# Moving the sample states' part of the delta rule beside the last prompt tile's gathers, and the cache pages to GpSimd's queue

## The reference

```python
q, k, v, qkv_b, z, b_raw, a_raw = project(rmsnorm(h), w_in)   # 1024 -> 3592 columns
oa = diff_attention(q, k, v)            # samples also read 8 pages x 128 keys and values of a paged cache each
q, k, v, g, beta = conv4_silu(qkv_b)    # four-tap causal convolution, then the decays
ob, S_new = gdn_chunk(S, q, k, v, g, beta)   # chunked delta rule; a sample sequence is one chunk of 8 tokens
#   rhs   = beta (v - e^G k S);  delta = solve(I + A, rhs)
#   ob    = e^G q S + (decay qk) delta
#   S_new = e^Gl S + delta^T (e^(Gl-G) k)
h = h + merge(oa, ob * silu(z)) @ w_out
# PEER: 8 heads choose 16 of 16384 experts each; one row of u and one of v per choice
h = h + sum_k gate_k gelu(xn . u[e_k]) v[e_k]
```

## Time and profile before

| | |
|---|---|
| runs, us | 2124.64, 2133.01, 2137.26 (median 2133.01) |
| profiled execution, us | 2127.18, of which the span is 2125.5 |
| busy | TensorE 81%, VectorE 63%, ScalarE 38%, GpSimd 37% |
| bytes | HBM read 762.27 MB, written 16.26 MB |
| first slot's dot product starts | 531.4 us into the span |

### The profile page before, as it was taken

The page is one execution under the profiler, slowest core; times in us unless marked ns, Lnnn a source line. Parts: engine busy times, 40 slices in busy tenths (PEclk is TensorE's granted clock), DMA queues, the critical chain, the costliest instruction groups (busy, mean ns, idle before and its releaser), DMA issues.

```text
span 2125.5 us, 20551 instructions
## 1 busy us (share of the span) xinstructions
PE 1728.4 (81%) x6211; PEld 864.8 (41%) x6211; DVE 1335.3 (63%) x3023; ACT 799.8 (38%) x2370; POOL 783.6 (37%) x704
## 2 busy tenths in 40 slices
PE   6886999998898887989788889978796667776877
PEld 1332454546453444445344435533452223443111
DVE  2333534334797656887665788865687876669654
ACT  1332321222544523563443345463243333323433
POOL 2132100012344443435334343634443554444442
PEclk8898999999998989999899999999897888888999
DMA  9797843226999999999999999999999999999997
GB/s 347 269 348 256 263 139 114 74 104 232 405 424 401 426 428 428 426 423 408 427 408 429 425 426 399 416 414 415 427 426 411 427 427 429 427 426 426 426 427 316
DMA packets 137479, 779.61 MB, mean 367 GB/s; under 512 B 14863, under 2 KB 23839, under 8 KB 59784
## 3 DMA queue, kind: packets, MB, share of 16 engines
q0 software_dynamic: 88384, 621.30, 70.3%
q1 hardware_dynamic: 45504, 149.69, 18.7%
q10 hardware_dynamic: 3480, 7.31, 0.9%
HBM read 762.27 MB, written 16.26 MB: 366 GB/s over the span
## 4 chain that ended last, share of the span: by engine, by line
PE 36%; DMA 34%; DVE 14%; ACT 7%; issue 4%; SPq 2%; POOL 1%; ACTq 0%; DVEq 0%; POOLq 0%
DMA sb_uv<-in_peer_uv,sb_eidx 29%; PE bank L2149 17%; DVE sb_uv L1747 6%; PE bank L1768 6%; PE bank L2116 3%; PE bank L2084 2%; DMA sb_xin<-pre_conv 1%; DMA sb_hres<-pre_conv 1%; ACT sb_diag L1326 1%; SPq L817 1%; ACT sb_ew L1319 1%; ACT L1315 1%; DMA pre_conv<-sb_raw 1%; DMA sb_zone<-in_w_route 1%; DVE sb_hres L1721 1%
## 5 line engine op out<-in xcount | busy, mean ns | idle before, releaser
L2149 PE MATMUL bank<-sb_uv,sb_diag 128*128 128x512 f32 (+1 forms) x1860 | 968.0, 658 | 306.2 <-ACT sb_diag L1326 296.2
L952 POOL DMA_INDIRECT sb_uv<-in_peer_uv,sb_eidx x576 | 692.3, 1202 | 897.1 <-PE bank L2149 682.5
L1747 DVE CUSTOM_DVE_ANT_0 sb_uv<-sb_uv,sb_xn 128x1024 f32<-128x1024 f32 x576 | 698.8, 1220 | 328.3 <-DMA sb_uv<-in_peer_uv,sb_eidx 325.9
L2149 PEld LDWEIGHTS bank<-sb_uv,sb_diag 128*128 128x128 f32 (+1 forms) x1860 | 341.4, 199 | 808.2 <-ACT sb_diag L1326 475.1
L1315 ACT ACTIVATE sb_gel<-sb_h 128x1 f32<-128x1 f32 x576 | 116.2, 202 | 800.4 <-DVE sb_h L1747 797.3
L1768 PE MATMUL bank<-sb_w,sb_xnT 128*128 128x512 f32 (+1 forms) x560 | 273.2, 632 | 25.7 <-DMA sb_w<-in_w_sections 14.9
L1326 ACT ACTIVATE sb_diag<-sb_stay,sb_ew 128x128 f32<-128x128 f32 (+1 forms) x465 | 183.2, 394 | 47.7 <-PE bank L2149 4.9
L1319 ACT ACTIVATE sb_ew<-sb_gel,sb_gate 128x1 f32<-128x1 f32 x576 | 169.7, 295 | 19.8
L2116 PEld LDWEIGHTS bank<-sb_rT,sb_zone 128*128 128x128 f32 x1280 | 155.6, 195 | 29.1 <-issue 28.7
L1768 PEld LDWEIGHTS bank<-sb_w,sb_xnT 128*128 128x128 f32 (+1 forms) x560 | 100.5, 191 | 153.3 <-issue 119.3
L2116 PE MATMUL bank<-sb_rT,sb_zone 128*128 128x128 f32 x1280 | 156.7, 278 | 2.1 <-issue 1.8
(11 more groups left out here) (347 smaller groups left out, 1540.3 us busy)
## 6 DMA issues: line engine op xcount, KB each, us to landing
sb_zone<-in_w_route SPq DMA_DIRECT2D x20, 2304.0 KB, 12.2
sb_w<-in_w_sections SPq DMA_DIRECT2D x40, 512.0 KB, 7.7
sb_zone<-in_w_mixer SPq DMA_DIRECT2D x10, 2048.0 KB, 16.5
sb_uv<-in_peer_uv,sb_eidx POOLq DMA_INDIRECT x576, 14.3
sb_sS<-in_cache_kT SPq DMA_DIRECT2D x24, 256.0 KB, 6.7
sb_zone<-in_cache_kT SPq DMA_DIRECT2D x24, 256.0 KB, 5.0
sb_sS<-in_cache_v POOLq DMA_DIRECT2D x24, 256.0 KB, 6.2
sb_hres<-pre_conv SPq DMA_DIRECT2D x4, 1024.0 KB
```

What stands on the lines that cost most here:

```text
L952: nc.gpsimd.indirect_dma_start(uv[:, m % RING, :], None, i["peer_uv"], bass.IndirectOffsetOnAxis(ap=eidx[:, t % 2, n:n + 1], axis=0)).then ...
L1747: nc.vector.tensor_tensor_reduce(out=uv[:, m % RING, 0:D], in0=uv[:, m % RING, 0:D], in1=xn2[:, t % 2, :], scale=1.0, scalar=0.0, op0=ALU. ...
L2149: ins = nc.tensor.matmul(bank[half][0:rows, :], lhsT=G["diag"][:, d % DIAGS, 0:rows], rhs=uv[:, m % RING, D + 512 * half:D + 512 * half + ...
```

## The change

- The samples' part of the delta rule leaves `gdn(0)`. What it still needs of `gdn(0)` (the arrays `wq`, `U`, `APT`, `kd` of the 64 sample rows) is spilled to DRAM and read back. `sample_states` and `sample_updates` run at slots 393 to 427, on a new scratch set `E` that lies over the zone of the routing weights; the states are loaded once the fourth tile's routing has freed that zone, and the mixer weights for the last tile wait until the new states are stored.
- The output of the meta tokens (lines 1950, 1951 for `gdn(0)`) is no longer computed.
- Cache pages, keys too, are loaded by GpSimd's queue (`page_loads`) into eight buffers: four for keys, four for values. Convolution rows get two buffers instead of four.
- Tokens, tables and biases of the front are loaded later; the small columns and the decay steps move into the first two `past` pairs.
- The front's due times are new, and three units instead of two come after the barrier.

```diff
-LATE = len(UNITS) - 2
+LATE = len(UNITS) - 3
-PAGE_BUFFERS = 6
+PAGE_BUFFERS = 8
...
 def unit_at(n):
-    if n < 4:
-        return early_at(22 + 6.9 * n)
-    if n < 15:
-        return early_at(55 + 10.4 * (n - 4))
+    if n < 5:
+        return early_at(22 + 6.9 * n + (1.4 if n == 4 else 0))
+    if n < 13:
+        return early_at(62 + 13 * (n - 5))
     if n < LATE:
-        return early_at(169.4 + 12.1 * (n - 15))
-    return -77 + 9.0 * (n - LATE)
+        return early_at(166 + 9.6 * (n - 13))
+    return -88.5 + 9.0 * (n - LATE)
...
-        return early_at((182, 284)[u] + (2.06, 2.15)[u] * k)
+        return early_at((192, 250)[u] + (2.06, 2.15)[u] * k)
+def sample_at(k):
+    return SLOTS * (PT - 1) + 9 + k
 def past_at(p, k):
-    return early_at(64 + 26 * p + k)
+    return early_at(58 + 27 * p + k)
...
-        conv_buffer = [m % 4 if m <= 2 * NT else (m + 1) % 2 for m in range(3 * NT)]
+        conv_buffer = [m % 2 for m in range(3 * NT)]
...
+                def sample_parts_out():
+                    yield gdn_at(0, 22.5)
+                    sp.wait_ge(s_uwc, 2)
+                    sp.wait_ge(s_at, 2)
+                    for part, dst in (...):
+                        sp.dma_start(dst, part).then_inc(s_ssp, 16)
+                def sample_parts_in():
+                    yield sample_at(-8)
+                    sp.wait_ge(s_s2p, 4 * PT)
+                    sp.wait_ge(s_ssp, 64)
+                    for src, dst in (...):
+                        sp.dma_start(...).then_inc(s_sS, 16)
                     for h in range(NH):
-                        yield past_at(NPAIR, 1 + 3 * h)
-                        sp.wait_ge(s_dpv, NPAIR)
-                        sp.dma_start(F["sS"][:, h, :, :], i["state_ssm"]...).then_inc(s_sS, 16)
+                        sp.dma_start(E["sS"][:, h, :, :], i["state_ssm"]...).then_inc(s_sS, 16)
...
                 def states_out():
                     for h in range(NH):
-                        yield gdn_at(0, 37 + 2 * h)
+                        yield sample_at(22 + 4 * h)
                         sp.wait_ge(s_snd, 3 * (h + 1))
...
                         elif part < 2:
-                            sp.wait_ge(s_s2p, 4 * (PT - 1) + part + 3)
+                            sp.wait_ge(s_sst, 16 * (NH + 1))
+                            sp.wait_ge(s_po, 2 * NT - 1)
+                            sp.wait_ge(s_dl, 2 * NT)
+                            sp.wait_ge(s_sn, NH)
...
-                def value_loads(p):
+                def page_loads(p, values, half):
+                    if p == 0:
+                        yield early_at((36.5, 44.8, 45.5, 64)[2 * values + half])
+                        pool.wait_ge(s_vecs, 128)
+                        pool.wait_ge(s_proj, 12 if values or half else 8)
+                        if values and half:
+                            pool.wait_ge(s_ss, NT)
+                    else:
+                        yield past_at(p - 1, 23 + half if values else 3 + 3 * half)
+                    for seq in range(2):
+                        pages = [...]                # four page numbers read into registers
+                        if values and p:
+                            pool.wait_ge(s_dpv, p)
+                        elif p:
+                            pool.wait_ge(s_ds, 2 * (p - 1) + half + 1)
+                        for g in range(4):
+                            pool.dma_start(cache_quarter(...)[:, g, :], cache[...]).then_inc(landed, 16)
...
+                def sample_states():                # on TensorE
+                    for h in range(NH):
+                        yield sample_at(3 * h)
+                        if h == 0:
+                            pe.wait_ge(s_sS, 16 * (NH + 4))
+                            pe.wait_ge(s_sTc, 1)
+                            pe.wait_ge(s_s2c, 4 * PT)
+                            pe.wait_ge(s_q2c, 4 * PT)
+                        ...                         # eight transposes
+                        yield sample_at(1.7 + 3 * h)
+                        ...                         # eight read-outs
+                    yield sample_at(13)             # then the turned result, and at 15.5 the output
                 def sample_updates(h):
-                    yield gdn_at(0, 35.5 + 2 * h)
+                    yield sample_at(17 + 4 * h)
```

More of the change, by code:

```diff
@@ L388, in hybrid_step @@
         s_gatea = sem("gate_steps_act")
-        s_cv = [sem(f"conv_rows_loaded{r}") for r in range(4)]
+        s_cv = [sem(f"conv_rows_loaded{r}") for r in range(2)]
         s_cw = sem("conv_weights_loaded")
@@ L559, in hybrid_step @@
         s_qt = sem("queries_loaded")
-        s_xTl = [sem(f"tokensT{'_and_cache_keys' if n < 2 else ''}_loaded{n}") for n in range(4)]
-        s_keys, s_vals = s_xTl[0:2], sem("cache_values_loaded")
+        s_xTl = [sem(f"tokensT_loaded{n}") for n in range(3)]
+        s_keys, s_vals = [sem(f"cache_keys_loaded{half}") for half in range(2)], sem("cache_values_loaded")
         s_qd = sem("sample_queries_spread")
@@ L830, in _ @@
                 work += [Stream(route_loads(n)) for n in range(NT)] + [Stream(residual_load(n)) for n in range(NT)] + [Stream(past_biases())]
-                work += [Stream(key_loads(p)) for p in range(NPAIR)] + [Stream(store(t)) for t in range(NT)]
+                work += [Stream(store(t)) for t in range(NT)]
                 advance(work, -200)
@@ new lines, in sample_states @@
+                def sample_states():
+                    for h in range(NH):
+                        yield sample_at(0.6 + 3 * h)
+                        for half in range(2):
+                            act.wait_ge(s_sT, 1 + 2 * h + half + 1)
+                            if h and half == 0:
+                                act.wait_ge(s_oT, h)
+                            nc.scalar.activation(E["sST"][:, 4 * half:4 * half + 4, :].rearrange("p b v -> p (b v)"), bank[(2, 6)[half]][:, :], ACT.Copy).then_inc(s_sTc, 1)
+                    yield sample_at(12)
+                    act.wait_ge(s_oT, NH)
+                    nc.scalar.activation(E["oT"][:, :, :, :].rearrange("p a h r -> p (a h r)"), bank[4][:, :], ACT.Copy).then_inc(s_oTc, 1)
@@ L1301, in _ @@
                 work = [Stream(xT_loads())] + [Stream(x_squares(n)) for n in range(NT)] + [Stream(unit_copy(n)) for n in range(len(UNITS))] + [Stream(turn_copy(u)) for u in range(2 * NT)]
-                work += [Stream(gates())] + [Stream(conv_silu(m)) for m in range(3 * NT)] + [Stream(gdn(u)) for u in range(NT)]
+                work += [Stream(gates())] + [Stream(conv_silu(m)) for m in range(3 * NT)] + [Stream(gdn(u)) for u in range(NT)] + [Stream(gdn_squares(u)) for u in range(NT)] + [Stream(sample_states())]
                 work += [Stream(attention_head(n, h)) for n in range(PT) for h in range(NH)] + [Stream(attention_squares(n)) for n in range(PT)]
@@ L1373, in gates @@
                     count.done(nc.vector.tensor_tensor(sgn[:, 0:1], sgn[:, 0:1], ea("first"), ALU.add), s_gate)
-                    yield early_at(72)
+                    yield past_at(0, 15.5)
+                    for n, (cols, b, many) in enumerate(((slice(0, SEQ), 2, SEQ), (slice(SEQ, TOK), 3, LAST))):
+                        dve.wait_ge(s_bac, n + 1)
+                        nc.vector.tensor_tensor(baT[:, cols], baT[:, cols], bank[b][0:2 * NH, 0:many], ALU.add).then_inc(s_bad, 1)
+                    yield past_at(0, 25)
                     dve.wait_ge(s_bac, 3)
@@ L1732, in _ @@
                 work = [Stream(xT_gains())] + [Stream(x_mean(n)) for n in range(NT)] + [Stream(gates())] + [Stream(conv(m)) for m in range(3 * NT)] + [Stream(qk_norm(u)) for u in range(2 * NT)]
-                work += [Stream(gdn(u)) for u in range(NT)] + [Stream(sample_updates(h)) for h in range(NH)] + [Stream(gdn_out(u)) for u in range(NT)]
+                work += [Stream(gdn(u)) for u in range(NT)] + [Stream(sample_delta())] + [Stream(sample_updates(h)) for h in range(NH)] + [Stream(gdn_out(u)) for u in range(NT)]
                 work += [Stream(attention_head(n, h)) for n in range(PT) for h in range(NH)] + [Stream(attention_norm(n)) for n in range(PT)]
@@ L2129, in _ @@
                 work = [Stream(unit(n)) for n in range(len(UNITS))] + [Stream(turn(u)) for u in range(2 * NT)] + [Stream(small_columns()), Stream(decay_totals())]
-                work += [Stream(gdn(u)) for u in range(NT)] + [Stream(sample_updates(h)) for h in range(NH)]
+                work += [Stream(gdn(u)) for u in range(NT)] + [Stream(sample_states())] + [Stream(sample_updates(h)) for h in range(NH)]
                 work += [Stream(attention_head(n, h)) for n in range(PT) for h in range(NH)] + [Stream(past(p)) for p in range(NPAIR)]
```

351 lines of the change are left out of this document (158 added, 193 removed).

## The result

The changed kernel takes 2165.86 us (median of 4 runs, 2165.50 to 2171.65), the kernel before 2133.68 beside it: a ratio of 1.016, 95% interval 1.013 to 1.019. It was forecast to take 2127, in a range of 2106 to 2150; it is slower than the kernel before and outside the range. The profiled execution has a span of 2163.9 us against 2125.5.

What follows compares the result with a forecast made beforehand. Bounds: TensorE in the front between 290 and 350 us, waits in the `past` stage, DMA bytes in the gather stage. Terms: −27 − 8 + 5 + 16 + 8 = −6 us, forecast 2127 us, range 2106 to 2150.

Steps and rivals of the forecast that it cites:

- part 2: `past` stage: ends at 223 instead of 246, a gain of 23 less 14.7 for two deferred units, 8 us.
- the 216 of the other terms: `past` stage: its end in us, with first scores at 64, before 7 was added for powers waiting behind pages.
- the fourth rival: `past` stage: GpSimd paces it fully, a pair takes 43 us or more; +17 us, 2150; chance 0.15.
- Parts 1 and 3: Front: 27 us of TensorE's work taken off; 5 us lost because `gdn(0)` needs the convolution of unit 13.
- Parts 4 and 5: Gather stage: 16 us for exposed bytes; 8 us lost as TensorE waits at slot 393 for state loads.
- part 4: Gather stage: states at 290 GB/s, 7.2 us each way, and 1.4 us for spilled parts; 16 us, all exposed.
- the forecast 1655: Gather stage: time in us near which the state loads finish and TensorE resumes at slot 393.
- The rival in which several small pieces pass at a time: Gather stage: state loads are in time, no wait at slot 393; −14 us, 2119; chance 0.23.
- by eight slots: Last tile: mixer weights, waiting for state stores until slot 444, are due at 452; otherwise TensorE waits up to 6 us.
- the front is shorter by under 20 us: Front: the prediction is wrong if it is shorter by under 20 or over 40 us.
- the hole: Gather stage: a hole in the DMA's GB/s near slot 393, some 8 us without gather data; absent, the prediction is wrong.

Runs made afterwards that it cites:

- e2: Changed kernel with the powers ahead of the next pair's key pages in GpSimd's order: 2148.75 us (1.007), stage end 227.
- e6: Changed kernel with one load for four page numbers on GpSimd, without the bounds instruction for each: 2125.78 us (0.997), stage end 212.
- e7: Changed kernel with both one load for four page numbers and the powers ahead of key pages on GpSimd: 2123.50 us (0.996), stage end 210.
- e14: Changed kernel with 56 unused columns behind its first buffer, gather ring at byte 160768: packets 309 ns; the columns alone gave 9 us.
- e9: Kernel before with eight unused columns behind its first buffer, gather ring at byte 160544: packets 315 ns, some 20 us over the kernel before.
- e16: Kernel before with 16 unused columns behind its first buffer, gather ring at byte 160576: packets 314 to 315 ns.
- e5: Kernel before, unchanged, run again as a control: 2131.97 us (0.999), packets 309 ns.
- e12: Kernel before with one load for four page numbers on SyncE and GpSimd: 2133.22 us (1.000).
- e4: Changed kernel with sample states loaded and stored in 4 KB pieces, not 512 bytes, so computing on permuted states: 2161.80 us (1.014).
- e8: Changed kernel with the sample states' work 16 slots later, their loads issued when they were: 2167.35 us (1.018).
- e10: Changed kernel with eight unused columns behind its first buffer, gather ring at byte 160576: packets 314 to 315 ns.
- e13: Changed kernel with 24 unused columns behind its first buffer, gather ring at byte 160640: packets 314 to 315 ns.

## Why the prediction was wrong

**The step that failed** is in part 2: "behind a `conv_rstd` that stands after 16 pages, VectorE waits up to 18 us, and behind it stands the next step of `past`. I add 7 for it: 223 instead of 246". The mechanism was named, the wait's length was nearly right (20.6 at the longest, four of them, 42.9 us), and its price was not: the stage ended at 250, so that over the 216 of the other terms it came to some 34. Not all of that is this term's: the first scores came 8 us earlier than forecast, at 55.6, and the first pair's 16.9 us of waiting for late convolution rows had no term. But the reading and the order of GpSimd's queue alone give back 23 to 40 us of the stage (e2, e6, e7). The waits don't lie beside each other. TensorE's transposes hang on `past_fold`, that on the norm, that on the power, the power on 32 pages (16 was my count; the next pair's keys stood there too), and the pages for the next value buffers on TensorE's products. I read this from the program's waits and the rows above: a ring, in which each turn pays in full. A pair took 54.2 and 48.3 us (key scores at 110.8, 165.0 and 213.3), over the 41 from which the fourth rival decides. That rival, "GpSimd paces it fully", is what happened; it had a chance of 0.15, and it put part 2 at +14.7, where the profiled executions give +19 (250 plus 14.7 for two deferred units, less 245.7). I had computed GpSimd's own 38.6 us a pair, against 43 available, and read the difference as slack. With other engines' results queued behind it, there was none.

**What no term had** is the place of the buffers: 15 us from slot 0 to 575 by the changed kernel against e14, 18 by e9 and e16 against the three of before. I read the move of the small table as a change of names. Nothing in the profile of before could show it; the diff did.

**Parts 1 and 3** (−27 and +5) held as a sum. From the start of the first unit behind the stage to the first dot product: 245.7 to 531.4 before, 249.9 to 530.6 after, which is 285.7 against 280.7. With 14.7 for the two deferred units the front shed 19.7 us, where 22 were forecast. This stretch varies between executions: it is 285.7 to 298.2 us, 292.9 on average, in five profiles with the front of before (before, e5, e9, e12, e16), and 280.6 to 286.4, 283.2 on average, in six with the changed front (changed, e4, e8, e10, e13, e14). By these averages 24.4 us were shed.

**Parts 4 and 5** (16 and 8) held as a sum. Slot 368 to 464 takes 290.5 us against 267.8 in e9, which has the same slow packets: 22.7. By e4 the small pieces and the wait are 10.3 of it and the rest 12.4. These are not parts 5 and 4: part 4 counted the small pieces at 290 GB/s, e4 takes away both that and the wait, and no run parts the two. The wait came at the place given, 19.32 us against some 20, and ended at 1661.4, 6 us after the forecast 1655; slot 368 was by then 6 us later than in the kernel before. The rival in which several small pieces pass at a time fell. That the mixer weights are hidden "by eight slots" held too: TensorE never waited for them. Their bytes moved: slots 384 to 400 took 53.4 us before, and in the changed kernel slots 432 to 448 take 54.3, where sixteen slots with nothing beside them take some 40.

**The sum** by the profiled executions: −6 as forecast, +27 for part 2, +15 for the place of the buffers, +2 for parts 1 and 3, −1 for 4 and 5: +37, against 38.4 of the spans. By medians the difference is 32, as the profiled execution of before was a quick one: its granted clock at 250 to 530 us was 0.99 where e5 has 0.96, and its first dot product came at 531.4 where e5 has 543.5. What sets the clock there is open. By the averages of the same five and six profiles the sum comes nearer to the medians. The stage ends at 248.3 before and 250.0 changed, which makes part 2 +16 in place of −8 and parts 1 and 3 −24 in place of −22. The front is then 8 us shorter (first dot product at 541.2 and 533.2), not equal, and with the place of the buffers at 15 to 18 the sum is +30 to +33. By either account the front is shorter by under 20 us, which the prediction named as its sign of being wrong; the hole, its other sign, was there.

Whether the work of the sample states is better placed beside the gathers at all is open: it trades some 20 us of the front for 23 of bytes and waiting, and no run undid it alone.

## What to carry to other kernels

A queue's own time against the time available is not its slack: list whose results stand behind its long entries, and if one of them leads back to what the queue waits for, count the whole stay, once a turn. Count register reads like DMA issues; they cost GpSimd as much here. Read four at a time, without the bounds instructions, they almost vanish, but that pays only where the queue sets the pace: in the kernel before it gave nothing. And when a change shifts the memory layout, look at where the buffer of the bound transfer now begins; a stretch that the change doesn't touch and that runs at another rate is the sign.

## What the runs showed of the hardware

- Gathers of 8 KB rows into a ring at byte 160512 or 160768 of a partition (multiples of 256) take 309 to 311 ns a packet, at 160544, 160576 or 160640 314 to 315: 427 against 420 to 422 GB/s late in the stage. With the ring every other buffer moved too. I had expected none of it, nor that multiples of 64 and 128 would not do.
- On GpSimd, four page numbers by four loads with their bounds instructions cost 2.25 us, as much as issuing four page DMAs (2.29); one load of four without them costs 0.42.
- Pieces of 512 bytes on SyncE's queue passed one for one with the packets of the gathers' queue, for loads (211 against 212 in 4 us, 187 of these rows of 8 KB) as for stores (156 against 154).
